# Attention outputs with the head in the inner loop, the last normalisation by half blocks on two engines, and ranking pieces spread over four steps

## The reference

```python
h = rms_norm(x, norm_mix)
q, k, v, cb, cc, cu, gates = split(h @ w_in)          # 8 heads of 64, 512 conv channels
att = stick_breaking_attention(q, k, v)               # strictly causal
y_a, y_b = att @ w_a, short_conv(cb, cc, cu) @ w_b
x = x + (sigmoid(ga) * y_a + sigmoid(gb) * y_b) @ w_o
q = rms_norm(x, norm_ffn) @ w_q                       # 8 heads x 2 halves x 128 keys
# per token and head: top 16 of either half, top 16 of the 256 sums, softmax gate,
# 16 of the 16384 experts: sum of gate * gelu(u . x) * v
x = x + peer(...)
return rms_norm(x, final_norm)
```

## Time and profile before

| | us |
|---|---|
| median of 3 runs | 1756.73 |
| the profiled execution's own time | 1754.75 |
| its span (first to last instruction) | 1753.0 |
| PE busy | 1709.8 (98%) |
| DVE busy | 1292.4 (74%) |
| ACT busy | 771.7 (44%) |
| POOL busy | 767.4 (44%) |

### The profile page before, as it was taken

The page is one execution under the profiler, slowest core; times in us unless marked ns, Lnnn a source line. Parts: engine busy times, 40 slices in busy tenths (PEclk is TensorE's granted clock), DMA queues, the critical chain, the costliest instruction groups (busy, mean ns, idle before and its releaser), DMA issues.

```text
span 1753.0 us, 24582 instructions
## 1 busy us (share of the span) xinstructions
PE 1709.8 (98%) x9066; PEld 1519.8 (87%) x9066; DVE 1292.4 (74%) x1844; ACT 771.7 (44%) x1092; POOL 767.4 (44%) x486
## 2 busy tenths in 40 slices
PE   7999999998999999999999999999999999999997
PEld 5778778887889999999999999999888888888885
DVE  2555511115999899989999789886787787787786
ACT  5444433234333566746667466654223323323322
POOL 3332334332311455665666578881533333332330
PEclk9999999999999999999999999999999999999998
DMA  5222223322235777777777988888999999999992
GB/s 156 73 60 84 60 73 95 108 73 72 84 118 191 221 247 247 240 251 283 259 248 254 327 306 299 292 305 318 376 370 377 360 346 378 361 357 360 368 343 103
DMA packets 212293, 413.80 MB, mean 236 GB/s; under 512 B 11504, under 2 KB 150800, under 8 KB 206864
## 3 DMA queue, kind: packets, MB, share of 16 engines
q1 hardware_dynamic: 156880, 253.78, 41.8%
q0 software_dynamic: 36864, 134.23, 21.4%
q10 hardware_dynamic: 18496, 25.19, 4.1%
HBM read 360.73 MB, written 52.43 MB: 236 GB/s over the span
## 4 chain that ended last, share of the span: by engine, by line
PE 80%; DVE 10%; POOL 3%; DMA 2%; ACT 2%; issue 2%; ACTq 0%; SPq 0%; DVEq 0%; POOLq 0%
PE psum L1205 28%; PE psum L229 22%; PE psum L1146 21%; PE psum L1136 4%; DVE ring L1468 2%; DVE ul L1393 2%; PE psum L1173 2%; DMA ring<-in_expert_u,index 1%; PE psum L303 1%; PE psum L289 1%; POOL ring L1352 1%; POOL grid L1371 1%; PE psum L423 1%; PE psum L317 1%; DVE hot L1456 1%
## 5 line engine op out<-in xcount | busy, mean ns | idle before, releaser
L1146 PE MATMUL psum<-xTh,uh 128*128 128x384 f32 x1024 | 354.1, 346 | 9.8 <-DVE ul L1393 9.3
L1146 PE MATMUL psum<-xTl,uh 128*128 128x384 f32 x1024 | 343.3, 335 | 0.0
L1146 PE MATMUL psum<-xTh,ul 128*128 128x384 f32 x1024 | 343.3, 335 | 0.0
L1352 POOL DMA_INDIRECT ring<-in_expert_v,index x128 | 176.9, 1382 | 311.0 <-DVE acc L1473 269.0
L212 POOL TENSOR_TENSOR wl<-raw,wh 128x1024 fp32r<-128x1024 f32 x72 | 172.5, 2403 | 320.9 <-ACT wh L485 320.9
L1205 PE MATMUL psum<-vh,dwh 128*128 128x512 f32 x768 | 298.8, 389 | 1.2 <-DVE dwl L1486 1.2
L1205 PE MATMUL psum<-vl,dwh 128*128 128x512 f32 x768 | 298.8, 389 | 0.0
L1205 PE MATMUL psum<-vh,dwl 128*128 128x512 f32 x768 | 298.8, 389 | 0.0
L1278 ACT ACTIVATE vh<-v_raw 128x4096 fp32r<-128x4096 f32 x31 | 112.6, 3634 | 340.2 <-PE psum L1205 339.8
L1352 POOL DMA_INDIRECT ring<-in_expert_u,index x128 | 172.9, 1351 | 152.6 <-DVE ring L1468 80.1
L1468 DVE SCALAR_TENSOR_TENSOR ring<-ring,x 128x1024 f32<-128x1024 f32 x120 | 199.8, 1678 | 12.3 <-DMA ring<-in_expert_u,index 11.0
(11 more groups left out here) (206 smaller groups left out, 2893.3 us busy)
## 6 DMA issues: line engine op xcount, KB each, us to landing
u_raw<-in_expert_u SPq DMA_DIRECT2D x128, 512.0 KB, 4.5
v_raw<-in_expert_v SPq DMA_DIRECT2D x30, 2048.0 KB, 12.2
expert_act<-hb ACTq DMA_DIRECT2D x128, 192.0 KB, 3.9
expert_gate<-grid SPq DMA_DIRECT2D x12, 2048.0 KB, 7.2
dh<-expert_act SPq DMA_DIRECT2D x32, 768.0 KB, 4.4
dg<-expert_gate SPq DMA_DIRECT2D x32, 768.0 KB, 6.7
raw<-in_w_in SPq DMA_DIRECT2D x40, 512.0 KB, 3.8
raw<-in_w_q SPq DMA_DIRECT2D x16, 512.0 KB, 4.0
```

Of the source, the lines that this page charges most:

```text
L1146: last = nc.tensor.matmul(zb[s][:, 0:DT], w[s][:, c, :], x[:, c, 0:DT], start=(c == 0 and i == 0), stop=(c == C - 1 and i == 2))
L1352: nc.gpsimd.indirect_dma_start(out=ring[k][:], out_offset=None, in_=tables[x // SLOTS], in_offset=bass.IndirectOffsetOnAxis(ap=index[:, x ...
```

## The change

Five things change; the diff below is cut to its core.

1. `outputs` waits for both heads and then takes them in turn within each key block.
2. Newton step: the factor -0.5 is put into the gains beforehand (`vecs`, `gain`, `fnorm`: one more DVE instruction each) and the last two instructions become one; in the tail the mean and the square are folded in as well.
3. Ranking pieces 4 to 23 are spread 5, 5, 5, 5 over steps 0 to 3 (before: 9, 6, 5 over steps 0 to 2). `x3`, all `keys` of the first two blocks, `address`, the gathers and the gates' exponentials come one step later, `gate_out` of the sparse block two steps, and the first gathered row moves from step 11 to 12 (step 84 takes one more).
4. `rows_done` divides by one less, so the rows of `expert_v` are finished within the last half round.
5. Tail: ACT squares by half blocks, right behind each add. For the last block DVE multiplies each half by `fnorm` before 1/rms is known; then DVE scales one half and ACT the other, and either half is sent by its own queue.

```diff
             pe.wait_ge(S["v_ready"], p + 1)
-            for e in range(2):
-                h = slice(e * HD, (e + 1) * HD)
-                pe.wait_ge(S["att_ready"], p * 2 + e + 1)
-                for kb in range(NB):
+            pe.wait_ge(S["att_ready"], p * 2 + 2)
+            for kb in range(NB):
+                for e in range(2):
+                    h = slice(e * HD, (e + 1) * HD)
                     last = nc.tensor.matmul(av[h, kb * P:], v[:, kb, h], z[:, e, ROW[kb]:ROW[kb] + T - kb * P],
...
-            chain(nc.vector.tensor_scalar(t, t, -0.5, 1.5, ALU.mult, ALU.add))
-            nc.vector.tensor_tensor(r, r, t, ALU.mult).then_inc(S["scales"], 1)
+            nc.vector.scalar_tensor_tensor(r, t, -3.0, r, ALU.add, ALU.mult).then_inc(S["scales"], 1)
...
-        nc.vector.tensor_copy(vecs[:], pj[0][:, 0:32]).then_inc(S["vec_in"], 1)
+        nc.vector.tensor_copy(vecs[:, 16:32], pj[0][:, 16:32])
+        nc.vector.tensor_single_scalar(vecs[:, 0:16], pj[0][:, 0:16], NEWTON, ALU.mult).then_inc(S["vec_in"], 1)
...
+        nc.vector.tensor_single_scalar(gain[:], gain[:], NEWTON, ALU.mult).then_inc(S["gain_in"], 1)
...
-KEYED = {SPARSE: (3, 4, 5, 6), 0: (7, 8, 9, 10)}
-GATED_IN = {4: (SPARSE, 0)}
-EXPS = {7: (SPARSE, 0)}
-GATED_OUT = {8: SPARSE, 11: 0}
+KEYED = {SPARSE: (4, 5, 6, 7), 0: (8, 9, 10, 11)}
+RANKED = (AHEAD, 9, 14, 19, 24)
+GATED_IN = {5: (SPARSE, 0)}
+EXPS = {8: (SPARSE, 0)}
+GATED_OUT = {10: SPARSE, 11: 0}
...
-    return IN_UP + 4 * z if z <= 2 else SLOTS + (z - 2) * SLOTS // (2 * ROUNDS - 2)
+    return IN_UP + 4 * z if z <= 2 else SLOTS + (z - 2) * SLOTS // (2 * ROUNDS - 3)
...
+        def square(b, half):
+            nc.scalar.activation(psum[:, 6 * T + half * T:7 * T + half * T], acc[:, b, half * T:(half + 1) * T], ACT.Square,
+                                 accum_out=ss[:, half, b:b + 1]).then_inc(Z["sq"], 1)
...
+        act.wait_ge(Z["scales"], NB)
+        nc.scalar.activation(acc[:, DB - 1, 0:T], last_block[:, 0:T], ACT.Copy, scale=rs[:, DB - 1:DB]).then_inc(Z["half"], 1)
+        act.wait_ge(Z["half"], 1)
+        act.dma_start(out[0, (DB - 1) * P:DB * P, 0:T], acc[:, DB - 1, 0:T]).then_inc(Z["out"], 16)
...
-            if n < 3:
+            if n < 4:
                 if n == 0:
                     dve.wait_ge(scores_out, LISTS + PRIMED)
-                for k in range((AHEAD, 13, 19)[n], (13, 19, 24)[n]):
+                for k in range(RANKED[n], RANKED[n + 1]):
...
+            nc.vector.scalar_tensor_tensor(va, ss[:, 0, b:b + 1], D * EPS, ss[:, 1, b:b + 1], ALU.add,
+                                           ALU.add).then_inc(Z["var"], 1)
+            dve.wait_ge(Z["root"], n + 1)
+            chain(nc.vector.reciprocal(r, r))
+
+            chain(nc.vector.scalar_tensor_tensor(t, va, r, r, ALU.mult, ALU.mult))
+            nc.vector.scalar_tensor_tensor(r, t, -3.0, r, ALU.add, ALU.mult).then_inc(Z["scales"], 1)
...
+        def weigh(half):
+            at, b = slice(half * T, (half + 1) * T), DB - 1
+            dve.wait_ge(Z["added"], 2 * b + half + 1)
+            chain(nc.vector.tensor_tensor(last_block[:, at], acc[:, b, at], fnorm[:, at], ALU.mult))
...
+        add(2 * DB - 2)
+        weigh(0)
+        add(2 * DB - 1)
+        weigh(1)
+        scale(NB - 1, DB - 1)
+        nc.vector.tensor_single_scalar(acc[:, DB - 1, T:D], last_block[:, T:D], rs[:, DB - 1:DB], ALU.mult).then_inc(Z["normed"], 1)
```

More of the change, by code:

```diff
@@ L43 @@
 FAR = -1.0e30
+NEWTON = -0.5
 KB = 1024
@@ L964, in rows_of @@
         return 1
-    return 3 if FIRST < n < FIRST + EVERY * 2 and t > 32 and t < 35 else 2
+    return 3 if FIRST < n <= FIRST + EVERY * 2 and t > 32 and t < 35 else 2
 def rows_done(n):
@@ L1027, in experts_program @@
     fnorm = m.put("fnorm", 100, [P, D])
-    fst = m.put("fst", 44, [P, 4, NB])
-    ss, var, rs, tmp = (fst[:, i, :] for i in range(4))
+    fst = m.put("fst", 44, [P, 5, NB])
+    ss = fst[:, 0:2, :]
+    var, rs, tmp = (fst[:, i, :] for i in range(2, 5))
+    last_block = ring[0]
     utp = psum[:, 6 * T:8 * T], psum[:, 0:2 * T]
@@ L1045, in experts_program @@
         [sem(f"d_{n}{i}") for i in range(2)] for n in ("v_in", "g_in", "h_in", "v_hi", "v_lo", "w_f", "w_hi", "w_lo", "mm_done"))
-    Z = {n: sem("d_" + n) for n in "fn_in sum_full sq root vchain normed out var added".split()}
+    Z = {n: sem("d_" + n) for n in "fn_in fn_neg sum_full sq root vchain scales normed half out var added".split()}
     hv = hd.rearrange("i (r s) t -> i r s t", s=2)
@@ L1326, in experts_scalar, with root @@
                     nc.scalar.activation(dots[:], dots[:], ACT.Gelu).then_inc(S["dot_act"], 1)
-        def norm(n, b):
-            nc.scalar.activation(psum[:, 6 * T:8 * T], acc[:, b, :], ACT.Square, accum_out=ss[:, b:b + 1]).then_inc(Z["sq"], 1)
+        def square(b, half):
+            nc.scalar.activation(psum[:, 6 * T + half * T:7 * T + half * T], acc[:, b, half * T:(half + 1) * T], ACT.Square,
+                                 accum_out=ss[:, half, b:b + 1]).then_inc(Z["sq"], 1)
+        def root(n, b):
             act.wait_ge(Z["var"], n + 1)
@@ L1334, in experts_scalar @@
         act.wait_ge(S["row_used"], 2 * SLOTS)
-        norm(0, SPARSE)
+        square(SPARSE, 0)
+        square(SPARSE, 1)
+        root(0, SPARSE)
         for b in range(DB):
-            act.wait_ge(Z["added"], 2 * b + 2)
-            norm(b + 1, b)
+            for half in range(2):
+                act.wait_ge(Z["added"], 2 * b + half + 1)
+                square(b, half)
+            root(b + 1, b)
+        act.wait_ge(Z["scales"], NB)
+        nc.scalar.activation(acc[:, DB - 1, 0:T], last_block[:, 0:T], ACT.Copy, scale=rs[:, DB - 1:DB]).then_inc(Z["half"], 1)
+        act.wait_ge(Z["half"], 1)
+        act.dma_start(out[0, (DB - 1) * P:DB * P, 0:T], acc[:, DB - 1, 0:T]).then_inc(Z["out"], 16)
     def experts_gpsimd(pool):
@@ L1554, in chain, with add @@
             dve.wait_ge(Z["vchain"], done[0])
-        def norm_out(n, b):
-            va, r, t = (x[:, b:b + 1] for x in (var, rs, tmp))
-            dve.wait_ge(Z["sq"], n + 1)
-            nc.vector.tensor_scalar(va, ss[:, b:b + 1], 1.0 / D, EPS, ALU.mult, ALU.add).then_inc(Z["var"], 1)
-            dve.wait_ge(Z["root"], n + 1)
-            chain(nc.vector.reciprocal(r, r))
-            chain(nc.vector.tensor_tensor(t, r, r, ALU.mult))
-            chain(nc.vector.tensor_tensor(t, t, va, ALU.mult))
-            chain(nc.vector.tensor_scalar(t, t, -0.5, 1.5, ALU.mult, ALU.add))
-            chain(nc.vector.tensor_tensor(r, r, t, ALU.mult))
-            nc.vector.scalar_tensor_tensor(acc[:, b, :], acc[:, b, :], r, fnorm[:], ALU.mult,
-                                           ALU.mult).then_inc(Z["normed"], 1)
-        dve.wait_ge(Z["fn_in"], 16)
-        norm_out(0, SPARSE)
-        for k in range(2 * DB):
-            if k % 2 == 0 and k:
-                norm_out(k // 2, k // 2 - 1)
+        def add(k):
             b, half = k // 2, k % 2
```

31 lines of the change are left out of this document (24 added, 7 removed).

## The result

The changed kernel takes 1747.21 us, the median of six runs (1745.33 to 1751.13), and the kernel before took 1756.8 beside it. The ratio is 0.9947 with a 95% interval of 0.9932 to 0.9962: faster by 9.3 us (6.7 to 11.9). Forecast were 12.3 us less, 1744.4, and 1740.8 to 1749.3 as the range.

What follows compares the result with a forecast made beforehand. PE, busy 1709.8 of 1753.0 us, was taken as the bound, with DVE and ACT ending the program. 4.65 - 1.0 + 0.4 + 2.85 + 5.4 = 12.3 us off 1756.73 gave 1744.4 us, range 1740.8 to 1749.3.

Steps and rivals of the forecast that it cites:

- Outputs in the loop: Three pairs' outputs on PE: both heads side by side take 2.30 instead of 3.85 us, 4.65 us won in all.
- The strict order: Rival at the outputs: column halves start in program order, 0.43 us lost in each of four places, 1746.1 us; chance 0.12.
- no overlap: Rival at the outputs: alternating heads do not overlap, 9.1 us lost in all, 1753.5 us; chance 0.04.
- exclusion: Rival at the outputs: alternating heads exclude each other, 6.9 us per pair, slower at 1762.9 us; chance 0.03.
- Outputs after the last pair: PE idles 3.96 us before the last pair's outputs and its clock may halve: -1.0 us, ends 0 and -1.65.
- Newton step: Norms: one chained instruction less, 0.20 us with its gap; 0.4 us won in all, ends 0.2 and 0.6.
- Ranking: Up phase, steps 0 to 12: ranking over four steps wins 2.85 us, ends 0 and 3.9.
- still fit into 5.06: Step 84: three rows and `ul` (3.7 + 1.1 us) fit into PE's step of 5.06 us without waits.
- the stall only moves: Rival in the up phase: PE pays the 2.85 us back in steps 9 to 12, 1747.3 us; chance 0.12.
- `expert_v` and tail: Program end: five last rows instead of nine bring DVE there 5.5 us earlier; tail wins 5.4 us, ends 2.4 and 6.2.
- the late tail: Rival at the end: tail stays with DVE by late `weigh` or costly queue, 3 us less, 1747.4; chance 0.08.

Runs made afterwards that it cites:

- both heads in one half: Changed kernel with the outputs of both heads of a pair summed into the same 64 partitions (attention output not the reference's); one execution, 1757.43 us.
- the second measurement: The changed kernel measured and profiled once more with no edit: 1748.26 us, ratio 0.9952 to the kernel before.
- The version without the two losses that could be mended: Changed kernel with two rows at step 13, two instead of three at step 84, and last pair's heads one behind the other: 1741.53 us, ratio 0.9921.

## Why the prediction was right in the main, and where it failed

**Outputs in the loop: right.** 1.58 us a pair by PE's lead (1.54 of it up to the start of `scores`), in every kernel with side-by-side heads; forecast 1.55. The strict order, which the forecast priced at 1.1 a pair, and the rivals of no overlap and of exclusion are out.

**Outputs after the last pair: the step mis-sized the clock.** The mechanism (the clock falls in the idle time that the change makes here) was right, the gap was right to 0.02 us, but the term "I take -1.0 us; ends 0 and -1.65" measured -3.8 in three traces, -3.6 in one and -1.8 in one, all outside its ends. I had read 3.3 us of half clock from the second norm, where PE worked without a break once it had begun. Here the outputs are followed by a second short wait (1.41 us for `atl`), and the clock stayed at half for 10.2 us; some 7.7 us of work at half rate cost 3.8. That the second wait is what drew it out is not shown: with the same two waits half clock lasted 3.4 us in two other traces (the old ranking order and both heads in one half). What differs is when the clock fell: 1.0 to 1.3 us before the outputs began in the four traces with 10.2 us, 0.2 to 0.3 us after they began in the two with 3.4. Why it falls at one time or the other stays open. The worst end of a clock's cost must cover all the work up to the next long unbroken stretch, not one recovery seen elsewhere.

**Newton step: right where it can be read, then lost again.** 0.2 us at the second norm, as forecast; the 0.2 at the start can't be read. The forecast took the time won ahead of the second norm as kept, but half clock ended there no earlier than before, so the region came out 0.5 slower.

**Ranking: right by step 12, and then mostly given back.** 2.84 us won by step 12 (63.81 us for steps 0 to 12), with the losses at the steps for which they were forecast: 0.40 at step 1, 0.45 at step 3, 0.41 at step 5, 0.70 at step 10. What failed is the sentence that the three rows of step 84 "still fit into 5.06". I had added busy times (3.7 + 1.1) and not asked whether the third row's gather is there. It had not landed. From step 11 to step 83 DVE has done one row fewer than before, and with a ring of five buffers (`RING`) each gather is issued one row later too; step 84 makes up the row on DVE, but its gather was issued only 5.5 us earlier. DVE waits 6.6 us in this stretch instead of 1.9, and PE loses 2.16 three and four steps later. So the rival "the stall only moves" holds for most of the 2.85 (the old order costs the same within the scatter, 1748.45), though not in its place: it named steps 9 to 12.

**Steps 51 and 52: not forecast at all**, -2.64 us in the profiled execution: a wait of 2.68 and some 1.7 for 3.4 us of work at half rate, less the 1.9 that these steps lose in the kernel before. Between step 12 and step 84 the prediction looked at no step.

**`expert_v` and tail: right.** 5.38 against 5.4; the last add 0.11 us behind PE, ACT's half 0.16 later than forecast. The split is new: 3.3 for the rows, 2.1 for the rest.

**The sum.** 12.3 - 2.8 (clock) - 0.9 (norms) - 2.2 (step 84) - 2.6 (steps 51, 52) + 0.1 (pairs) = 3.9 for the profiled execution, the difference of the two spans. By the medians 9.3 to 9.6 were won, and 8.1 in the second measurement. That the first of these come within some 3 us of the forecast is in part luck, since the losses that it left out or sized too small are 8.4 us in the trace. Why the medians show less of them isn't shown. The granted clock, known for every execution, does not do it: of the first six the one with the highest (0.997) took 1749.19 us, one with the lowest (0.994) 1745.39. The version without the two losses that could be mended came to 14.4 (by its interval 11.4 to 16.2), where the forecast without its 1.0 for the clock is 13.3.

One figure of the prediction does not follow from its terms: the upper end of the range. The moved stall (1747.3) with the strict order, 1.7 more, gives 1749.0, and with the late tail, 3 more, 1750.3; the 1749.3 is neither.

## What to carry to other kernels

Put products of different halves of the output columns next to each other in PE's queue, but only where their operands are all there: behind a wait, let the part that is ready go first, even if it wins nothing by itself, since here it kept the clock. When work leaves one step, look where a table puts it back, and read there not only the busy time but whether its gathers have landed. And compare several traces of one kernel before a wait is charged to a change.

## What was not expected of the hardware

- Overlap of the column halves is nearly complete: 2.31 us for both heads, 2.37 busy for one alone, 4.46 for two in one half.
- The clock held over idle gaps of 2.80 and 1.61 us at full pace, and fell at one of 3.98; once down it stayed at half for 10.2 us in four traces and for 3.4 in two, of nearly the same program. After a wait of 2.68 us at step 52 it was at half for 3.4 us (the 0.59 over 4 us above), and after waits of 2.5 us there in three other traces too, so gaps shorter than the harmless 2.80 of step 1 did cost clock.
- DVE and POOL held each other up by nearly the whole instruction. POOL began its subtraction at 786.36 and took 1.90; DVE's row, begun at 786.70, ended at 789.34, which is 1.08 after POOL's end, for a row of 1.23; in the three other traces with this loss it was 1.08 too. With DVE first (786.38, 1.22), POOL's subtraction of 1.90 took 2.74. The Trainium skill (SBUF — State Buffer, Who interferes with whom, and SBUF: two separate sides) says that a DVE instruction with two inputs in SBUF and a GpSimd one that reads SBUF exclude each other: whichever starts first has the shared ports for the whole instruction, and the other blocks. The traces agree to 0.2 us (the second ends that much sooner than full exclusion would have it), and add that here it matters who is first: PE waits for what follows DVE's row within the step, and not for POOL's subtraction.
